# Query and key columns of a first-stage attention branch turned by DMA instead of by TensorE

## The reference

```
u = rmsnorm(h, mix_norm)
qa, ka, va, qb, kb, vb, qi, ki, wi, g = split(u @ w_in)      # 8 heads of 64 columns each for a and b
qa = rmsnorm(qa, q_norm_dsa);  ka = rmsnorm(ka, k_norm_dsa)  # per head, over its 64 columns
qb = rmsnorm(qb, q_norm_moba); kb = rmsnorm(kb, k_norm_moba)
out_a = dsa_attention(qa, ka, va, qi, ki, wi, bias_dsa)      # keys chosen by top 64 of index scores from qi, ki, wi
out_b = moba_attention(qb, kb, vb, bias_moba)                # at 256 tokens: one block, plain causal attention
h = h + (sigmoid(g_a) * (out_a @ w_a) + sigmoid(g_b) * (out_b @ w_b)) @ w_out
```

## Time and profile before

| | |
|---|---|
| median of 3 runs | 998.8 us (998.78 to 998.86) |
| profiled execution | 998.68 us, of which the span from first to last instruction is 996.9 us |
| PE | 990.9 us busy, 4626 matmuls |
| weight load of PE | 813.0 us |
| DVE | 688.2 us, 1009 instructions |
| ACT | 548.4 us, 752 instructions |
| POOL | 116.0 us, 109 instructions |

### The profile page before, as it was taken

How to read it: one execution, slowest core, us unless ns; L and a number is a source line. 1 busy time by engine, 2 the same in 40 slices (tenths; PEclk the granted TensorE clock), 3 DMA queues, 4 the chain that set the end, 5 groups by cost and what they waited for, 6 DMA issues and landing times.

```text
span 996.9 us, 12571 instructions
## 1 busy us (share of the span) xinstructions
PE 990.9 (99%) x4626; PEld 813.0 (82%) x4626; DVE 688.2 (69%) x1009; ACT 548.4 (55%) x752; POOL 116.0 (12%) x109
## 2 busy tenths in 40 slices
PE   9999999999999999999999999999999999999998
PEld 7788888888877888888888878888888888888887
DVE  6766566668987667656666677797689767656663
ACT  7444343576765546444343576768885555443541
POOL 0000000022200000000000041168914000000000
PEclk9999999999999999999999999999999999999999
DMA  8987776585443546666656376457555546787761
GB/s 264 291 256 254 236 247 211 194 309 175 144 152 130 170 140 202 227 213 203 224 186 228 125 259 211 148 170 211 149 188 197 205 152 207 232 218 225 231 191 43
DMA packets 158985, 199.87 MB, mean 200 GB/s; under 512 B 49617, under 2 KB 105050, under 8 KB 158810
## 3 DMA queue, kind: packets, MB, share of 16 engines
q1 hardware_dynamic: 158922, 199.24, 62.2%
q10 hardware_dynamic: 16, 0.00, 0.0%
HBM read 182.45 MB, written 5.77 MB: 189 GB/s over the span
## 4 chain that ended last, share of the span: by engine, by line
PE 97%; DMA 2%; ACT 1%; SPq 0%; issue 0%; DVE 0%; ACTq 0%
PE bank L1897 23%; PE bank L1899 23%; PE bank L1898 23%; PE bank L2005 7%; PE bank L2003 7%; PE bank L2004 7%; PE bank L1912 1%; PE bank L2054 1%; DMA raw<-in_w_in 1%; PE bank L2168 1%; DMA raw<-in_ffn_w_gu 0%; PE bank L2069 0%; PE bank L2056 0%; PE bank L2126 0%; PE bank L2289 0%; PE bank L2290 0%
## 5 line engine op out<-in xcount | busy, mean ns | idle before, releaser
L1897 PE MATMUL bank<-hi,xh 128*128 128x512 f32 (+1 forms) x944 | 375.2, 397 | 1.0 <-DVE lo L1515 0.6
L1899 PE MATMUL bank<-hi,xl 128*128 128x512 f32 (+1 forms) x944 | 367.3, 389 | 0.0
L1898 PE MATMUL bank<-lo,xh 128*128 128x512 f32 (+1 forms) x944 | 366.5, 388 | 0.0
L1277 DVE TENSOR_TENSOR lo<-raw,hi 128x2048 fp32r<-128x2048 f32 (+1 forms) x111 | 254.0, 2289 | 146.7 <-ACT hi L799 146.6
L799 ACT ACTIVATE hi<-raw 128x2048 fp32r<-128x2048 f32 (+1 forms) x114 | 216.6, 1902 | 133.4 <-PE bank L2005 96.9
L1897 PEld LDWEIGHTS bank<-hi,xh 128*128 128x128 f32 x944 | 177.3, 188 | 39.7 <-issue 3.3
L1899 PEld LDWEIGHTS bank<-hi,xl 128*128 128x128 f32 x944 | 177.2, 188 | 37.4
L1898 PEld LDWEIGHTS bank<-lo,xh 128*128 128x128 f32 x944 | 177.5, 188 | 34.3
L1294 DVE TENSOR_TENSOR lo<-raw,hi 128x1024 fp32r<-128x1024 f32 (+1 forms) x108 | 133.1, 1243 | 40.7 <-ACT hi L808 40.1
L2003 PE MATMUL bank<-hi,hh 128*128 128x512 f32 x304 | 118.9, 391 | 0.0
L2005 PE MATMUL bank<-hi,hl 128*128 128x512 f32 x304 | 118.4, 389 | 0.0
(11 more groups left out here) (265 smaller groups left out, 963.1 us busy)
## 6 DMA issues: line engine op xcount, KB each, us to landing
raw<-in_w_in SPq DMA_DIRECT2D x48, 1024.0 KB
raw<-in_ffn_w_gu SPq DMA_DIRECT2D x82, 512.0 KB
raw<-in_ffn_w_down SPq DMA_DIRECT2D x22, 1024.0 KB
raw<-in_w_up SPq DMA_DIRECT2D x16, 1024.0 KB
raw<-in_w_down SPq DMA_DIRECT2D x16, 1024.0 KB
raw<-in_w_out SPq DMA_DIRECT2D x8, 1024.0 KB
distance_table<-ftab SPq DMA_DIRECT2D x8, 576.0 KB
raw<-in_w_proj_attn SPq DMA_DIRECT2D x4, 1024.0 KB
```

What stands on the lines that cost most here:

```text
L1277: nc.vector.tensor_tensor(lo[s][:, :, 0:width], raw[s][:, :, 0:width], hi[s][:, :, 0:width].bitcast(F32), ALU.subtract).then_inc(lo_done, 1)
L1897: nc.tensor.matmul(o, sh, wh, start=first and j == 0, stop=False)
L1898: nc.tensor.matmul(o, sh, wl, start=False, stop=False)
L1899: ins = nc.tensor.matmul(o, sl, wh, start=False, stop=last and j == 3)
```

## The change

The query and key groups c = 1 and 2 (`q_m`, `k_m`: in the code the buffers of the block branch, though the change is named after the indexed one) are no longer transposed by PE. The parts:

1. `M1_T` loses steps 9, 10, 13 and 14: 16 transposes on PE, four copies with a norm vector on ACT.
2. ACT writes the 16-bit planes of `hid[:, t]` into space of `gates1`, at steps 8, 9 (q) and 12, 13 (k).
3. SP turns them with four DMA transposes of 128 x 1024 16-bit elements: q's two after both loads of group 4 (units 8 and 9), k's two after both loads of group 6 (units 12 and 13).
4. DVE merges the planes of q at step 12, after waiting for both of q's DMAs. ACT merges those of k at step 16, after waiting for both of k's DMAs.
5. DVE multiplies the two norm vectors into one column once, at the start; ACT multiplies `q_m` by it in place at step 14. `k_m` gets none.
6. ACT's evacuations wait for the planes of the group before instead of for PE's transposes; the first scores wait for the merge of k; counts of `m_trev` are renumbered.

```diff
-M1_T = {(0, 0): 6, (0, 1): 7, (1, 0): 9, (1, 1): 10, (2, 0): 13, (2, 1): 14,
-        (4, 0): 21, (4, 1): 22, (5, 0): 25, (5, 1): 26}
+M1_T = {(0, 0): 6, (0, 1): 7, (4, 0): 21, (4, 1): 22, (5, 0): 25, (5, 1): 26}
+M1_PLANES = {8: 0, 9: 1, 12: 2, 13: 3}
+M1_MERGE = (12, 16)
+M1_GAIN = 14
...
+            def flip_first(c):
+
+                for t in range(NT):
+                    sp_eng.wait_ge(ffns[0].planes, 2 * (NF1 - 1) + 2 * (c - 1) + t + 1)
+                    sp_eng.dma_start_transpose(m_turned_planes_of(c)[:, :, t * P:(t + 1) * P],
+                                               m_planes_of(c, t)).then_inc(ffns[0].flip[t], 16)
+
             for c, (first, width, _) in enumerate(IN1):
                 for half in range(2):
                     columns(a["w_in"], U_M1 + 2 * c + half, first, half, width=width)
+                if c in (4, 6):
+                    flip_first(1 if c == 4 else 2)
...
+                if p in M1_PLANES:
+                    m = M1_PLANES[p]
+                    act.wait_ge(m_qn, m + 1)
+                    nc.scalar.activation(m_planes_of(1 + m // 2, m % 2).rearrange("p (s c) -> p s c", s=2),
+                                         hid[:, m % 2, :].bitcast(U16).rearrange("p (c s) -> p s c", s=2),
+                                         ACT.Copy).then_inc(ffns[0].planes, 1)
+                if p == M1_GAIN:
+                    act.wait_ge(ffns[0].merged, NF1)
+                    act.wait_ge(cols_done, 5)
+                    step(nc.scalar.activation(q_m[:, :, :], q_m[:, :, :], ACT.Copy,
+                                              scale=cols[:, C_GAIN + 2:C_GAIN + 3]))
+                if p == M1_MERGE[1]:
+                    for tt in range(NT):
+                        act.wait_ge(ffns[0].flip[tt], 16 * (NF1 - 1) + 32)
+                    nc.scalar.activation(k_m[:, :, :].bitcast(U16).rearrange("p k (c s) -> p s k c", s=2),
+                                         m_turned_planes_of(2).rearrange("p (s k) c -> p s k c", s=2),
+                                         ACT.Copy).then_inc(ffns[0].merged, 1)
...
+                dve.wait_ge(cols_done, 4)
+                g = C_GAIN + 2
+                nc.vector.tensor_tensor(cols[:, g:g + 1], cols[:, g:g + 1], cols[:, g + 1:g + 2],
+                                        ALU.mult).then_inc(cols_done, 1)
...
+                if p == M1_MERGE[0]:
+                    for tt in range(NT):
+                        dve.wait_ge(ffns[0].flip[tt], 16 * (NF1 - 1) + 16)
+                    nc.vector.tensor_copy(q_m[:, :, :].bitcast(U16).rearrange("p k (c s) -> p s k c", s=2),
+                                          m_turned_planes_of(1).rearrange("p (s k) c -> p s k c", s=2)
+                                          ).then_inc(ffns[0].merged, 1)
...
-                        pe.wait_ge(m_trev, 6)
+                        pe.wait_ge(ffns[0].merged, NF1 + 1)
```

More of the change, by code:

```diff
@@ L307, in program, with m_planes_of, m_turned_planes_of @@
                 otl = sb("otl", [P, 8, SEQ], F32R, s2)
+        def m_planes_of(c, t):
+            return gates1[:, c - 1, t * W:(t + 1) * W].bitcast(U16)
+        def m_turned_planes_of(c):
+            return gates1[:, c - 1, 2 * W:4 * W].bitcast(U16).rearrange("p (k c) -> p k c", c=SEQ)
         lamv = pt2[:, 0, 0:4 * HD].rearrange("p (a b) -> p a b", b=HD)
@@ L1026, in _ @@
                     else:
[L1027 to L1030, removed]
+                        dst = {4: q_a, 5: k_a}[cc]
+                        g = {4: 0, 5: 1}[cc]
                         nc.scalar.activation(dst[:, :, tt * P:(tt + 1) * P],
@@ L1066, in _ @@
                         m = 2 * (1, 2, 4, 5).index(c) + t
-                        if m >= 2:
-                            act.wait_ge(m_tr, m + 1)
+                        if m >= 6:
+                            act.wait_ge(m_tr, m - 3)
+                        elif m >= 2:
+                            act.wait_ge(ffns[0].planes, 2 * (NF1 - 1) + m - 1)
                         nc.scalar.activation(hid[:, t, :], G[t][:, :], ACT.Copy, scale=rstd).then_inc(m_ev, 1)
@@ L2146, in _ @@
                     if k == NH:
-                        pe.wait_ge(m_trev, 10)
+                        pe.wait_ge(m_trev, 6)
                     qt, kt = (q_m, k_m) if k < NH else (q_a, k_a)
```

## The result

The changed kernel takes 1010.84 us in the median of four runs (1010.21 to 1010.88), the kernel before 998.79 (998.19 to 998.86, four runs): a ratio of 1.0124 [1.0112, 1.0136]. The forecast was 1010.3, with a range of 1006.5 to 1013.0. The profiled run took 1010.88 us with a span of 1009.0.

What follows compares the result with a forecast made beforehand. PE, busy 990.9 of 996.9 us, was taken to bound the kernel. Its shift, max(9.2 bank wait + 2.3 clock, 10.4 DVE path) = 11.5 us, on 998.8 gave 1010.3 us; range 1006.5 to 1013.

Steps and rivals of the forecast that it cites:

- The four groups: Steps 9, 10, 13, 14: removing four groups of four PE transposes saves 0.44 us each, 1.76 us in all.
- The first stall: Before step 16, PE waits 1.5 us for ACT's late evacuation of v; 0.2 us of the removed transposes are left.
- DVE and the load: DVE's q merge takes 1.33 us, unheld by q's DMAs; unit 13's load, waiting for DVE's step 16, issues at 246.0.
- The landing: k's DMAs, awaited by ACT in step 16, land at L + 7.6 = 253.6; L is unit 13's load issue, 246.0.
- Rival 2: k's two back-to-back DMAs behind a load land late, at L + 11: 14.9 us, total 1013.6; chance 0.07.
- Rival 1: k's DMAs land fast, at L + 4.05, 3.55 us earlier: total 1006.7; chance 0.09.
- ACT's merge: In step 16, ACT's 128 x 2048 merge of k's planes takes 1.91 us.
- PE's restart: PE starts step 20 at 258.15, 9.2 us later than before, when ACT has evacuated group 4's first bank.
- The clock: Behind the step 20 stall PE runs 5.1 us at half speed, costing 2.3 us more (ends 0 and 3).
- Rival 4: The clock does not fall, or recovers at once: DVE's path decides, 10.4 us, 1009.1; within the 0.80 for 1008 to 1012.5.
- DVE's path: Head sums of step 18 come 10.9 us late; with 0.5 us of room, this alone holds PE 10.4 us.
- The shift stays to the end, since PE waits for nothing there.: After step 23: PE's shift of 11.5 us stays unchanged to the kernel's end.

Runs made afterwards that it cites:

- k_planes_after_v: Changed kernel with k's transposes before unit 11's load, both merges on ACT in step 16, gain at step 20, k's second planes at step 15: 996.82 us.
- k_flip_early: Changed kernel with SP issuing k's two DMA transposes before unit 11's load instead of behind unit 13's: 998.09 us, ratio 0.9998.
- fill_stall: Changed kernel with 88 extra PE transposes of the identity into an unused bank behind step 19: 1009.47 us, ratio 1.0108.
- before_again: The kernel before, unchanged, run once more under a new name for a second profile: 998.50 us, ratio 1.0000.
- before_plus_dve_copy: The kernel before with one extra 128x2048 16-bit copy on DVE in step 12, of the q merge's shape: 998.93 us, ratio 1.0004.
- before_fewer_transposes: The kernel before without 12 of the 16 PE transposes of q_m and k_m: 996.60 us, ratio 0.9982.

## Why the prediction was right, term by term

All the signs that it named for the changed trace came: ACT's wait to 253.9 for the DMA, PE's longest wait released by the bank, the clock below full behind it, the transposes behind a load at 246.2, the first stall, and no idle time of DVE before the merge of q.

**The four groups, 1.76 us.** Three of them are gone at 232.0, where PE leads by 1.41 less the offset 0.15: 1.26, 0.42 a group (0.44 forecast). k_planes_after_v, which has no stall before step 16, leads by 1.86 at 238.1 with its offset taken off.

**The first stall, 1.5 us.** An idle 1.76, the start at 238.00 instead of 238.09: with the offset, nothing of the removed transposes is left, where 0.2 was forecast. ACT's order was as worked out: planes at 233.14, gain at 236.00, v at 237.17. The gain took 1.13, not 1.05.

**DVE and the load.** The merge of q took 1.35 (1.33 forecast), began at 233.03 without a wait, and the load of unit 13 went out at 245.80 (246.0 forecast).

**The landing.** 253.6 forecast as L + 7.6; it was 253.85, L + 8.05. The second transpose held SP for 4.31 us where the earlier trace rows had 1.84. It stood right behind the first, and so only 1.7 us behind the load. The trace of before has both cases already: three pairs of one form behind a load in the second mixing stage, and a pair in the SwiGLU loop, of half the size, that was issued 1.30 us apart but over 6 us behind the last load:

```profile
L648 SPq DMA_TRANSPOSE late_t<-ig x3: 1837/2277/3647, 648.0 to 688.2; - x3
36.52 2.50 SPq L516 DMA_TRANSPOSE halves_t<-halves  x2
```

The three held SP 1.84, 2.28 and 3.65 us and were issued 3.41, 3.11 and 2.43 us behind their load (2.92, 2.62 and 1.94 behind the first of the pair): the closer, the longer. The pair of the SwiGLU loop held it 1.20 us each. So, as far as the smaller size allows the comparison, to follow at once is not enough; the load close in front belongs to it. Rival 2 had named both, with the wrong size: its L + 11 did not come, for SP's wait lies inside the time to landing (6.34 us from the issue). Rival 1, the fast landing, is refuted right behind a load. Farther behind one it is what one sees: k_flip_early's two transposes, issued 3.3 and 7.6 us behind the last load, landed 3.0 and 2.7 us after their issue. Of q's transposes the prediction said that they are issued seven steps of DVE work ahead of their merge; it was 12 us (220.98 to 233.03), or about four steps.

**ACT's merge, 1.91 us.** The one term mis-sized by much: 2.48 us, 0.57 more. I had taken the f32 full-unit copy over twice the plane copy (2.1), and both are below it.

**PE's restart.** 258.15 forecast, 258.98 measured: +0.57 from the merge and +0.25 from the landing make up all but 0.01 of the 0.83.

**The clock, 2.3 us.** It fell at 251.2, 2.4 us after PE's last matmul began, and was full again at 264.8, 5.8 us after the restart. From 10.01 to 12.87 us of shift it cost 2.86 us, near the end of the range (3). fill_stall shows it the other way: clock full, no such step. Rival 4, that it does not fall, is refuted by the 0.50 of 258 to 262, and "TensorE: Matmul & The Clock Gate", Part 1, of the Trainium skill is borne out: the stall cost more than its length.

**DVE's path, 10.4 us.** The second logits came at 273.17 against 261.48, 11.7 late, or 11.2 counting the 0.5 of room as the prediction did. It did not decide, as forecast, but was only 1.4 us away by fill_stall, where it decides.

**"The shift stays to the end, since PE waits for nothing there."** This step failed, by 0.7 us: from 580 to 590 the shift goes from 12.89 to 12.17. The kernel before has a stall that I had not looked for, at the start of the second mixing stage; here first PE of before, then ACT of before and ACT of k_flip_early:

```profile
589.14 0.39 PE L1899 MATMUL bank<-hi,xl 128*128 128x512 f32 x1
589.96 0.47 PE L1897 MATMUL bank<-hi,xh 128*128 128x512 f32 x1 [0.43 <-ACT hid L1163]
```

```profile
587.60 1.06 ACT L808 ACTIVATE hi<-raw 128x1024 fp32r<-128x1024 f32 x1 [1.53 <-DMA raw<-in_w_in]
```

```profile
586.11 1.06 ACT L829 ACTIVATE hi<-raw 128x1024 fp32r<-128x1024 f32 x1
```

It is there in before, before_again and before_plus_dve_copy, and gone in before_fewer_transposes and in all kernels that have the change. ACT waits in it for a load. In the traces of before and before_again an instruction fetch (16 KB, about 1 us) runs on the same DMA engines at 583.4; in k_flip_early it comes at 587.2. It goes the same way in all twelve traces: the three with the stall (before_plus_dve_copy's is at 583.8, that is 583.4 with its shift of 0.35 taken off) have the fetch there, and the nine without it have it 4 us later or more. That is still a coincidence in time, and no run moved the fetch alone: the cause stays open.

**The sum.** 9.2 + 2.3 = 11.5 forecast; measured 10.0 + 2.9 = 12.9, less 0.7: 12.2, which is the distance of the two profiled times. Two misses of opposite sign (+1.4 and -0.7) brought the total nearer than its terms: that it came within 0.6 us is in part luck. The mechanism is shown apart from the total: k_flip_early takes the wait away, and the loss goes with it.

## What to carry to other kernels

A wait belongs to the engine whose queue it blocks, so price it by all that stands behind it: the same late DMAs cost PE 10 us and a slow clock when ACT waited ahead of two halves and a bank, 2.5 us (in the profiled run) when it waited behind them, and nothing when SP issued them ahead of unit 11's load. Trace the wait back to the instruction that lets the transfer be asked for, before looking at how long the transfer takes. Work added to the next engine shows on the bounding one as soon as it is more than that engine's room (here about 0.8 us of DVE's), while without added work PE kept its whole gain of 1.3 us: put added work on the engine that is idle there in its own order, not on the one that is idle on average.

## What the runs showed of the hardware

- A 128x2048 copy of 16-bit elements that writes them interleaved took ACT 2.48 to 2.54 us; the 128x2048 f32 copy into `hi` takes 1.91. DVE does the first in 1.35.
- Two DMA transposes issued back to back: the first holds SP 1.24 us, the second 4.3 (4.20 to 4.42 in the eleven such pairs of first-stage transposes in eight traces, all right behind a load), against 1.84 when it came 2.9 us behind the earlier trace rows. In k_flip_early the second of k came 4.3 us behind the first and 7.6 us behind the last load, with the DMA engines idle, and held SP 1.23. With no load close in front, following at once did not lengthen the hold (1.20 us, at half the size).
- A copy on POOL of 2.99 us stopped a DVE instruction with two inputs for 2.27 us.
- A stall of 10 us cost 2.86 us more by the clock, which was at its half level for 5.8 us after the restart.
